# A state space mixer's scan in blocks of four times, on one core

## The reference

```
u = h @ w_in                                  # 256 times x 1024 channels = 64 groups x 16
a = exp(lam * dt)                             # complex, for 64 groups x 64 states
B' = f * b ,  f = (a - 1) / lam               # complex weights, 16 inputs per group
x[t] = a * x[t-1] + B' u[t]                   # complex state, for each group and state
y[t] = Re(C x[t]) + d_skip * u[t]             # 16 outputs per group
y = gelu(y);  y = y * sigmoid(y @ w_glu);  out = y @ w_o
```

## Time and profile before

| | us |
|---|---|
| median of 3 runs | 3051.48 (3048.74 to 3052.8) |
| profiled execution, its own time | 3046.99 |
| its span | 3045.2 |
| PE busy | 2875.2 (94%) |
| DVE busy | 1949.0 (64%) |
| ACT busy | 1331.5 (44%) |
| POOL busy | 356.7 (12%) |
| mean granted TensorE clock | 0.973 of full |

### The profile page before, as it was taken

How to read it: one execution, slowest core, us unless ns; L and a number is a source line. 1 busy time by engine, 2 the same in 40 slices (tenths; PEclk the granted TensorE clock), 3 DMA queues, 4 the chain that set the end, 5 groups by cost and what they waited for, 6 DMA issues and landing times.

```text
span 3045.2 us, 42524 instructions
## 1 busy us (share of the span) xinstructions
PE 2875.2 (94%) x17340; PEld 2525.8 (83%) x17341; DVE 1949.0 (64%) x2163; ACT 1331.5 (44%) x1326; POOL 356.7 (12%) x250
## 2 busy tenths in 40 slices
PE   6988998887999999999999999999999999998999
PEld 4868987357888888888787899888899999996999
DVE  5474443974888898889553663587466476566664
ACT  1222332003776677667443442243544354335443
POOL 1002941950000000000000100011100010001000
PEclk8969999998999999999999999999999999999999
DMA  7854575014989999999554364433356455572553
GB/s 241 275 160 145 190 239 152 0 56 167 370 309 334 337 367 326 334 337 368 183 203 162 119 193 131 156 119 111 111 170 206 153 166 193 172 180 92 170 183 108
DMA packets 491968, 608.21 MB, mean 200 GB/s; under 512 B 37337, under 2 KB 358972, under 8 KB 491836
## 3 DMA queue, kind: packets, MB, share of 16 engines
q1 hardware_dynamic: 490512, 605.51, 59.8%
q10 hardware_dynamic: 1324, 0.80, 0.1%
HBM read 605.22 MB, written 1.05 MB: 199 GB/s over the span
## 4 chain that ended last, share of the span: by engine, by line
PE 77%; DVE 9%; DMA 5%; issue 5%; ACT 3%; DVEq 0%; SPq 0%; POOL 0%; ACTq 0%
PE bank L1231 30%; PE bank L1724 7%; PE bank L1091 5%; PE bank L1570 4%; PE bank L1574 4%; DMA ring<-in_o_exp_down 4%; PE bank L1583 4%; PE bank L1500 3%; PE bank L1119 3%; DVE std L3186 2%; DVE ring L2769 1%; PE bank L1193 1%; PE bank L1505 1%; PE bank L1197 1%; ACT store_area_r L2481 1%
## 5 line engine op out<-in xcount | busy, mean ns | idle before, releaser
L2869 DVE TENSOR_TENSOR ring_r<-ring,store_area_r 128x2048 fp32r<-128x2048 f32 (+1 forms) x344 | 803.0, 2372 | 226.9 <-ACT store_area_r L2111 224.1
L2111 ACT ACTIVATE store_area_r<-ring 128x2048 fp32r<-128x2048 f32 (+1 forms) x344 | 666.0, 1971 | 241.4 <-PE bank L1231 81.3
L1231 PE MATMUL bank<-sq_r,store_area_r 128*128 128x256 f32 x1648 | 241.5, 288 | 13.0 <-ACT sq_r L2115 8.0
L1231 PE MATMUL bank<-sq_r,ring_r 128*128 128x256 f32 x1664 | 235.5, 285 | 0.0
L1231 PE MATMUL bank<-hT_r,store_area_r 128*128 128x256 f32 x1648 | 233.0, 284 | 0.0
L1017 POOL TENSOR_TENSOR silu_g<-silu_g 128x768 f32<-128x768 f32 (+2 forms) x14 | 29.9, 2136 | 1731.5 <-ACT silu_g L2123 1352.6
L1231 PEld LDWEIGHTS bank<-sq_r,store_area_r 128*128 128x128 f32 x1648 | 217.1, 193 | 18.6 <-issue 9.0
L1724 PE MATMUL bank<-hT,ring 128*128 128x256 f32 x1024 | 230.0, 380 | 0.0
L3277 DVE TENSOR_TENSOR ring_r<-ring,store_area_r 128x3072 fp32r<-128x3072 f32 x64 | 195.0, 3087 | 54.3 <-ACT store_area_r L2481 54.3
L1231 PEld LDWEIGHTS bank<-sq_r,ring_r 128*128 128x128 f32 x1664 | 216.5, 193 | 0.0
L1231 PEld LDWEIGHTS bank<-hT_r,store_area_r 128*128 128x128 f32 x1648 | 214.5, 194 | 0.0
(11 more groups left out here) (498 smaller groups left out, 4925.0 us busy)
## 6 DMA issues: line engine op xcount, KB each, us to landing
ring<-in_o_exp_gate SPq DMA_DIRECT2D x88, 1024.0 KB, 7.2
ring<-in_o_exp_up SPq DMA_DIRECT2D x88, 1024.0 KB, 7.3
ring<-in_ffn_w_gu SPq DMA_DIRECT2D x88, 1024.0 KB, 6.8
ring<-in_o_exp_down SPq DMA_DIRECT2D x32, 1536.0 KB, 8.5
ring<-in_ffn_w_down SPq DMA_DIRECT2D x32, 1408.0 KB, 9.3
ring<-in_o_exp_down SPq DMA_DIRECT2D x32, 1280.0 KB, 11.3
ring<-in_ssd_w_in SPq DMA_DIRECT2D x32, 1024.0 KB, 7.3
ring<-in_e_mod_mix_w SPq DMA_DIRECT2D x12, 1024.0 KB, 8.8
```

The lines of the kernel that those rows point to most:

```text
L1231: i = mm(out, w(k), x(k), start=(p == k == 0), stop=(p == 2 and k == blocks - 1))
L2111: activation(dst, slot(u, s, kk), ACT.Copy).then_inc(w_high, 1)
L2869: nc.vector.tensor_tensor(slot(u, s, kk, rounded=True), slot(u, s, kk), as_f(high), ALU.subtract).then_inc(w_low, 1)
```

## The change

The scan is cut into blocks of four times. u is rearranged so that the times 4k + j of one j lie together ("phase" j, 64 times each), and four groups of 32 channels side by side; the state is kept for every fourth time only.

- **Weights times powers.** B' is multiplied with a^3, a^2, a and 1 for the four phases, so one product of 128 rows gives the input of a whole block, and C with 1, a, a^2, a^3 likewise for the output. What a time gets from times of its own block comes from a *direct* product: small 128 x 128 matrices made from B and C with powers.
- **Scan.** 8 steps (`S5_M`) in place of 32. A step holds four old tiles with 64 times each: the turn (1024 elements), eight scans of 64 in place of two of 256, the product with the cosines (512), and a new combine (two operations of 256) on VectorE; GpSimd's two adds and product as before. The tables have 64 times a tile, a quarter of before. TensorE has 8 products for the inputs and 12 for the outputs of a step, all of 64 columns or 63. TensorE's order is `inputs(m + 2)`, then `outputs(m)`.
- **Moves.** u is rearranged by 32 transfers from SBUF to SBUF (`inputs_moved`), y back by 16 a step (`outputs_moved`), half of them issued by SP and half by ScalarE.
- **Preparation.** GpSimd makes the powers (`s5_weights`: small columns, then B in two halves of 16 tiles with 32 operations of 256 elements each, then tables, then C together with VectorE). TensorE has 64 transposes of B in 16 chunks after gates 3, 4, 5, 6, 10 and at modulation 16, and 16 of C after the first down unit; ScalarE copies each chunk. The raw B is loaded in halves by SP behind the weights of gates 3 and 8 (the second half waits for GpSimd), raw C behind modulation 17, and raw B once more in `s5_in`.
- **Direct products** stand in `s5_in`: blocks 0 to 5 after the first input unit, 6 and 7 after the second, eight products of 128 columns each, with four ScalarE copies a block.
- **Experts.** `outputs_low(0)` moves ahead of the differences of the last down unit; for more than 128 tokens the first unit's last pass for the first half of the tokens moves ahead of the gather.

```diff
+    S5_L = 4
+    S5_B = T // S5_L
+    S5_M = NS // 4
+    BT_AFTER = {3: (0, 1), 4: (2, 3), 5: (4, 5), 6: (6, 7), 10: (8, 9, 10, 11)}
...
+    def outputs_moved(eng, issue, m, phases):
+        eng.wait_ge(moved[m % 2], MOVES * (m // 2 + 1))
...
+        for j in phases:
+            for b in range(4):
+                issue.dma_start(y_nat(m)[32 * b:32 * b + 32, j * S5_B:(j + 1) * S5_B],
+                                y_raw(m)[32 * j:32 * j + 32, b * S5_B:(b + 1) * S5_B]).then_inc(moved[m % 2], 16)
...
# SP, even FFN
+                        if i in (3, 8):
+                            b_half_in((3, 8).index(i))
...
# GpSimd, even FFN
+                pool.wait_ge(unit_done, Unit(base["even_ffn"]).at(1))
+                fill(store_area[:, 48 * T:64 * T], 0.0)
+                def b_powers(h):
+                    pool.wait_ge(raw_in, 48 + 32 * (h + 1))
...
+                    for j in range(S5_L):
+                        f_re, f_im = (s5_over(b_factor(j) + n, 16 * h, 16, 16) for n in range(2))
+                        tally.up(gps.tensor_tensor(t[0], b_half[0], f_re, ALU.mult))
...
+                        for g in range(2):
+                            for n in range(2):
+                                ins = gps.tensor_tensor(s5_bw[n][part, :, j, 16 * g:16 * g + 16], ...
...
# TensorE
+            def b_turned(c):
+                pe.wait_ge(bw_ready, h + 1)
+                bank = chunk_bank(c)
+                for b in range(4):
+                    i = nc.tensor.transpose(...)
...
+                def direct(m):
+                    bank = d_banks[m % 2]
+                    if m >= 2:
+                        pe.wait_ge(bc_cp, before + m - 1)
+                    pe.wait_ge(c_powers, 4 + m)
+                    for b in range(4):
+                        for n in range(2):
+                            ins = mm(bank[:, b * P:(b + 1) * P], b_rows(m)[:, n, b, :], ...
+                def outputs(m):
...
+                    pe.wait_ge(back_c, m + 1)
...
                 wide(Unit(first), KD, h, h_of("om"))
-                (transposes of B)
+                for m in range(6):
+                    direct(m)
                 wide(Unit(first + 1), KD, h)
-                (transposes of C, loop over 32 steps)
+                inputs(0)
+                inputs(1)
+                for m in range(6, S5_M):
+                    direct(m)
+                for m in range(S5_M):
+                    if m + 2 < S5_M:
+                        inputs(m + 2)
+                    outputs(m)
...
# ScalarE, s5_in
+                unit_in(0)          # copy of the unit, then its 8 moves
+                se.wait_ge(c_powers, 3)
+                for m in range(6):
+                    direct(m)
...
+                for m in range(S5_M):
+                    se.wait_ge(w_used, m + 1)
+                    activation(y_raw(m), y_banks[m % 2][:, 0:T], ACT.Copy).then_inc(y_cp, 1)
+                    outputs_moved(se, nc.scalar, m, (2, 3))
+                    if m >= 2:
+                        gelu(m - 2)
...
# VectorE, scan
+                for m in range(S5_M + 5):
+                    # m < 8: turn m; 1 <= m: scans and cosines of m-1; 2 <= m: combine of m-2 -> back_c
+                    # m >= 5: add d_skip * u for m-5, once its moves have landed
...
# experts
                     for i in range(1, DN_UNITS):
+                        if i == 3:
+                            outputs_low(0, e)
                         down_low_parts(i, e)
...
                     gather_low(e + 1)
-                    outputs_low(0, e)
```

More of the change, by code:

```diff
@@ L385, in program @@
[L385 to L393, removed]
@@ L749, in modulation, with glu_units, s5_units @@
                     load(u, s, w)
-            def s5_products(stage):
+            def glu_units(first, last):
+                s5_units("s5_glu", S5_UNITS[first:last])
+            def s5_units(stage, units):
                 w = w3(dict(s5_glu="o_w_glu", s5_out="o_w_o")[stage], 0)
-                for st, at, kind, i in S5_UNITS:
-                    if st == stage and kind == "mod":
+                for _, at, kind, i in units:
+                    if kind == "mod":
                         modulation(Unit(base[stage] + at), i)
-                    if st == stage and kind != "mod":
+                    if kind != "mod":
                         u = Unit(base[stage] + at)
@@ L1457, in s5_in @@
-                pe.wait_ge(y_read, 8)
+                before = BT_CHUNKS + C_CHUNKS
+                def direct(m):
[3 more added lines that the diff above has]
+                    pe.wait_ge(c_powers, 4 + m)
+                    for b in range(4):
+                        for n in range(2):
+                            ins = mm(bank[:, b * P:(b + 1) * P], b_rows(m)[:, n, b, :],
+                                     s5_ct[n][:, 4 * m + b, :, :].rearrange("p j c -> p (j c)"), start=(n == 0), stop=(n == 1))
+                    ins.then_inc(bc_tr, 1)
@@ new lines, in inputs @@
+                def inputs(m):
+                    pe.wait_ge(moved[m // 4], MOVES)
+                    if m >= 2:
+                        pe.wait_ge(bu_turned, m - 1)
+                    for b in range(4):
+                        for n in range(2):
+                            ins = mm(v_banks[m % 2][:, n * T + b * S5_B:n * T + (b + 1) * S5_B], s5_bt[n][:, 4 * m + b, :],
+                                     u_rel(m)[:, b * S5_B:(b + 1) * S5_B], start=True, stop=True)
+                    ins.then_inc(bu_ready, 1)
@@ L2107, in even_ffn, with b_copied, c_copied @@
                         high(i + 1, 1)
+                    for c in BT_AFTER.get(i, ()):
+                        b_copied(c)
+                for c in range(12, BT_CHUNKS):
+                    b_copied(c)
+                se.wait_ge(bw_ready, 3)
+                for c in range(C_CHUNKS):
+                    c_copied(c)
+            def b_copied(c):
+                m, n = divmod(c, 2)
+                se.wait_ge(bc_tr, c + 1)
+                activation(s5_bt[n][:, 4 * m:4 * m + 4, :].rearrange("p i s -> p (i s)"), v_banks[c % 2][:, :], ACT.Copy).then_inc(bc_cp, 1)
+            def c_copied(c):
+                n, half = divmod(c, 2)
+                se.wait_ge(bc_tr, BT_CHUNKS + c + 1)
+                bank = v_banks[c % 2][:, :].rearrange("p (i c) -> p i c", c=32)
+                i = slice(16 * half, 16 * half + 16)
+                for g in range(2):
+                    part = slice(64 * g, 64 * g + 64)
+                    activation(c_small[n][part, i, :], bank[part, :, 16 * g:16 * g + 16], ACT.Copy)
+                activation(s5_ct[n][:, i, 0, :], bank, ACT.Copy).then_inc(bc_cp, 1)
             def high_part(u, s, kk, dst):
@@ L2351, in s5_in @@
                 norm("om")
[L2352 to L2362 removed]
+                first = base["s5_in"]
@@ L2363, in s5_in, with direct, gelu @@
+                def direct(m):
+                    se.wait_ge(bc_tr, BT_CHUNKS + C_CHUNKS + m + 1)
+                    bank = d_banks[m % 2][:, :].rearrange("p (i c) -> p i c", c=P)
+                    for j in range(S5_L):
+                        part = slice(32 * j, 32 * j + 32)
+                        ins = activation(s5_direct(m)[part, :, 32 * j:P], bank[part, :, 0:P - 32 * j], ACT.Copy)
                     ins.then_inc(bc_cp, 1)
-                for m in range(8):
+                def gelu(m):
@@ L3148, in s5_in @@
+                t = [silu_g[:, n, :].rearrange("p (i k) -> p i k", k=16) for n in range(2)]
                 for n in range(2):
```

503 lines of the change are left out of this document (346 added, 157 removed).

## The result

The changed kernel takes 3123.58 us (median of 4 runs, 3121.66 to 3126.07), beside 3050.11 for the kernel before (4 runs, 3045.55 to 3052.8): ratio 1.0247, 95% interval 1.0233 to 1.0262. It is 2.5% slower where 0.9% faster was forecast. The profiled execution has a span of 3122.1 us, 76.9 more than before.

The account below looks back on a forecast made before the run. TensorE was taken as the bound outside the scan, VectorE and GpSimd together inside it. Terms -38.4 + 9.6 + 14 - 13.7 = -28.5 us gave 3018.5 profiled, 3023 predicted; own range 3005 to 3038, overall 2982 to 3052.

Parts of the forecast that it names:

- I let everything behind shift together: Experts: no product waits for a weight transfer itself, so removing TensorE's 12.4 us of waits shortens everything behind.
- -13.7 us: Experts: 12.4 us of waits for VectorE's output half go, and 1.3 us in the expert with 256 tokens.
- 20 x 0.218 + 0.3 = 4.7: Scan loop: TensorE's share of a step, 20 products at the low clock plus 0.3, 4.7 us of a 10.4 us step.
- 16 input products 1.8 us: Mixer before the scan loop: input products after the second input unit take 1.8 us, first combine at about 543.
- a block 1.45 us, 8 transfers 3.5 us: Before the scan loop: ScalarE's copies per direct block and its issues; sixth block ends about 12.4 us after the first unit.
- -38.4: Whole mixer: -41.4 us from the new scan, plus 3 us for GLU's slow clock.
- The serial loop, its low clock and VectorE's part: Scan loop: VectorE 5.7 us, then TensorE 4.7 at the low clock, in turn; 10.4 us a step.
- The even FFN: Work moved there: +9.6 us for 80 transposes and +14 for stall and clock, 23.6 together.
- The stall: Even FFN after gate 3: TensorE waits 12 us for GpSimd's powers of B, ready at 328.7; bounds 0 and 25.
- GpSimd did not bind: Rival: GpSimd's powers of B become the bound; at 2.0 us an operation 3066 us; chance 0.10.
- The output moves: Rival: 128 output moves bound the scan loop, 1.5 us an issue, step 12.9, 3044 us; chance 0.10.
- The experts' weights: Rival: the weights stream binds the experts, so the 13.7 us stay lost, 3037 us; chance 0.08.

Follow-up runs that it names:

- e2: The kernel before with only the two reorder edits to the experts; 3030.96 us, ratio 0.9939.
- e1: The changed kernel with 24 one-column memsets added on VectorE ahead of the experts; 3049.46 us, ratio to the kernel before 0.9999.
- e6: The kernel before with 170 one-column memsets on VectorE ahead of the experts; 3118.38 us, ratio 1.0224.
- e4: e1 plus a third PSUM bank for the scan inputs, so TensorE computes inputs a step further ahead; 3015.09 us, ratio 0.988.
- e10: e1 with 32 in place of 64 columns in each scan input product; 16 passes took 3.57 us against 3.62; whole time 3182.21 us, one run.
- e9: e1 with ScalarE's 8 issues of the first inputs moved behind its copies of the six direct blocks; 3039.59 us, ratio 0.9968.
- e8: e4 with two products of 512 columns, on data nobody needs, added to each scan step; 3002.65 us, ratio 0.9853.

## Why the prediction was wrong, step by step

- **"I let everything behind shift together"** is the step that failed first, with "The 12.4 us of TensorE waits go: -12.4. ... -13.7 us". The waits went (e2: the reorder alone is worth 16.4 us in the experts). But the change has other instructions ahead of the experts, so VectorE's loop there lies elsewhere, and six of its seven jumps cost the kernel 11.5 us each (111.0 against 99.5 from expert to expert): +55 us in place of -13.7. e1 takes it away with 24 idle instructions, e6 makes it in the kernel before. I had listed what every engine does, and not where its code stands. The Trainium skill has the rule ("Runtime: NRT & Kernel Launch", Instruction fetch mechanics): code comes in blocks of 256 instructions into a window of two, and a branch out of the window stalls until its block is fetched. The runs agree that branches are what stalls: the jump back and the branch to the code for at most 128 tokens each had their stand and their packets. They do not show the block's size: 698 and 953, 255 records apart, both stall and 893 doesn't, which a period of 128 gives too. The loop is some 264 records long with the code of both branches. By an estimate from that section's window of two blocks of 256, a loop of this length would stall only where it reaches into a third block, at 7 starts of 256. Two neighbouring bad places and three free ones fit that, but no run looked for the bounds.
- **"20 x 0.218 + 0.3 = 4.7"**, TensorE's part of a scan step, is a mis-sized term: it measured 9.0. The duration was right, 0.214. But 6.97 us for "x32" is 32 passes, two for each f32 product, and I took them for 32 products: a step has 40 passes, not 20. In the loop this is 5 x (15.09 - 10.4) = 23 us, in the outputs after it 8 more (667.8 - 650.2 = 17.6 against 9.7). e4 shows the passes by themselves, e10 that their columns don't set them. The same slip is in the eight direct products of a block (16 passes; the six blocks took 11.6 us in e9, not 5.4) and in "16 input products 1.8 us" (32 passes, 3.7 us).
- **"a block 1.45 us, 8 transfers 3.5 us"** ahead of the loop: an issue took 0.70 us, not 0.43, and a block's copies 1.75, so that the direct blocks ended 18.2 us after the first unit, not 12.4: +6. The second unit ran at the full clock (13.98 us): -3. The first combine came 3 us later than summed, 1.9 of it by the input passes: +3. From the last output to GLU the forecast had 11.8 us with the slow clock. It was 8.1, because ten passes of GLU's first unit ran before the last GELU was done: -4. With the 23 and 8 us above this makes +33, so -5 in place of -38.4.
- **The serial loop, its low clock and VectorE's part** were right: 6.1 us against 5.7 (scans 2.54, forecast 2.3; product 0.69, forecast 1.01; the combine 1.30 + 0.41 where GpSimd's product runs beside it, forecast 0.9). The clock was 0.50 through the loop. That agrees with the Trainium skill's rule that bursts with waits between them start cold ("TensorE: Matmul & The Clock Gate", Part 1, HAM oscillation); e4 goes beyond the rule, with the clock at 0.50 and hardly a wait.
- **The even FFN** was right in its mechanism and nearly in its terms, but that +26 lies so near to +23.6 is in part luck: 4.5 of the 26 had come before gate 3, so 21.5 belong to the terms. The stall was 9.3 from start to start, not 12, and the slow gate behind it 1.7, not 2. The raw half landed at 298.0, not 293.5, but gate 3 ended as much later, at 320.8; GpSimd's 32 operations took 32 us, not 35. The chunks after gates 3 to 6 added 4.2 (forecast 3.5), the group after gate 10 2.5 (2.4), the chunks of C 3.8 (3.7). The mean of 1.0 us an operation was close to the forecast's 1.1, though no operation took that: the port rule that the prediction names is what the five long ones show, and without them the powers would by estimate (330.1 less five times 2.0) have been ready at 320, when gate 3 was done.
- **The rivals.** None of them is what happened. GpSimd did not bind (1.0 us an operation). The output moves did not set the step: ScalarE's eight issues took 5.3 us of 15.1, it waited for TensorE before them, and e4's step fell to 8.5 with the same moves. The experts' weights did not take the 13.7 (e2). The slower side got 0.10 for another cause, GpSimd. Two sums are off by little: GpSimd at 2.0 us gives 3067, not 3066, and the range's upper end by its own terms 3047, not 3052; 3123.58 lies outside either way. Without the stand of VectorE the change would be e1, 3049.5, no difference: the pass count alone had eaten the forecast gain.

## What to carry to other kernels

A loop that an engine runs with jumps has a place in its code, and anything added or removed ahead of it moves it, and with it the branches inside; look for "issue" waits right behind the loop's last line and for the packets of the instruction queue before blaming the edit, and try a few dozen idle instructions. When a duration is taken from a grouped row, find out whether its count is of products or of passes, by a row whose source is known. A serial chain between two engines is worth more to break (15.1 to 8.5 us here, with one more bank) than any of its parts is to shorten.

## What the runs showed that I had not expected

- Six jumps of one loop cost VectorE 68 us, and TensorE 52.7 in waits for it, in two parts each: 5.1 to 5.5 us behind the jump back and 6.2 behind the branch to the other half of the body, with five code packets to each jump. At three other places there was none of it. What a packet holds, the period of the places and the bounds of the bad ones are open.
- A GpSimd operation of 0.62 to 0.75 us took 2.7 when it met a VectorE product with two inputs in SBUF, five times of five, and ended 0.5 to 0.6 us after that product.
- TensorE busy 29.3 of 30 us with passes of 64 columns had a granted clock of 0.50; two products of 512 columns in each step of 20 narrow ones, on data nobody reads, brought it to 1.00 and took 8 to 12 us off the kernel (e8 against e4).
- A pass with a full 128x128 f32 weight takes 0.214 us at 1.2 GHz, at 32 and at 64 columns alike, and 0.11 at 2.4 GHz with 64.
